# Two attention blocks: VectorE's weight subtractions moved up, fixed PSUM banks in the late rounds, GpSimd held at two points

## The reference

```python
h = rms_norm(x, attn_pre_norm[l])
proj = h @ w_in                      # 16 tiles of 128 columns, and tokens' values
o_fox = fox_attention(...)           # 4 heads, causal, with forget gates
o_dil = dilated_attention(...)       # 4 heads, three patterns
o_nsa = g0 * o_compressed + g1 * o_selected + g2 * o_window   # 8 heads, 2 kv groups
x = x + rms_norm(concat(o_fox, o_nsa, o_dil) @ w_out, attn_post_norm[l])
h = rms_norm(x, ffn_pre_norm[l])
x = x + rms_norm(conv_ffn(h), ffn_post_norm[l])
```

## Time and profile before

| | |
|---|---|
| median of 3 runs | 2835.21 us (2833.09 to 2837.86) |
| the profiled execution's own time | 2833.32 us |
| its span, first to last instruction | 2831.5 us |
| TensorE busy | 2719.4 us, 96% of the span |
| VectorE, ScalarE, GpSimd busy | 47%, 46%, 46% |
| mean granted TensorE clock | 0.993 of full |
| attention rounds and output product, layer 0 and 1 | about 2132 to 2264 us and 2496 to 2628 us |

### The profile page before, as it was taken

One profiled execution on the slowest core, in us unless ns is written; L12 is line 12 of the kernel. 1 busy time (PEld: TensorE's weight loads), 2 busy tenths in 40 slices (PEclk: granted clock), 3 DMA queues, 4 the chain that ended last, 5 costly groups with the idle time before them and its releaser, 6 DMA issues.

```text
span 2831.5 us, 42503 instructions
## 1 busy us (share of the span) xinstructions
PE 2719.4 (96%) x17634; PEld 2311.0 (82%) x17634; DVE 1329.0 (47%) x2629; ACT 1290.5 (46%) x2189; POOL 1294.6 (46%) x584
## 2 busy tenths in 40 slices
PE   7999999899999999999999999999999999999999
PEld 5777877688887687887878879989988699886997
DVE  2678867641333311103767664453126554156541
ACT  3254543423523522224464445654455566554664
POOL 3332021134442444442831428758860178720787
PEclk9999999999999999999999999999999999999999
DMA  6332012123233434334520215535553355543455
GB/s 244 103 130 101 31 67 82 53 99 117 90 127 122 164 134 149 118 99 148 180 82 16 83 61 179 171 108 185 178 194 118 114 160 182 166 145 112 151 184 156
DMA packets 104072, 361.40 MB, mean 128 GB/s; under 512 B 11142, under 2 KB 18566, under 8 KB 103368
## 3 DMA queue, kind: packets, MB, share of 16 engines
q1 hardware_dynamic: 103880, 358.68, 38.2%
HBM read 357.59 MB, written 1.05 MB: 127 GB/s over the span
## 4 chain that ended last, share of the span: by engine, by line
PE 83%; DVE 9%; ACT 4%; DMA 1%; POOL 1%; issue 1%; SPq 0%; DVEq 0%; ACTq 0%
PE PS L385 82%; DVE PS L2127 1%; DVE AR L2119 1%; ACT AR L1386 1%; DVE AR L2317 1%; POOL RINGL L2984 1%; DVE SM L2391 1%; ACT XT L1386 1%; DVE RINGL L2119 1%; PE PS L396 1%; DVE XT L2119 1%; DVE AR L2123 0%; POOL HTR L2989 0%; ACT L1386 0%; DVE AR L2410 0%
## 5 line engine op out<-in xcount | busy, mean ns | idle before, releaser
L2984 POOL TENSOR_TENSOR RINGL<-RING,WH 128x1024 fp32r<-128x1024 f32 x516 | 1229.3, 2395 | 1470.0 <-ACT WH L1366 1449.3
L1366 ACT ACTIVATE WH<-RING 128x1024 fp32r<-128x1024 f32 x548 | 569.5, 1045 | 689.9 <-PE PS L385 563.1
L385 PE MATMUL PS<-HTR,WH 128*128 128x256 f32 (+2 forms) x2736 | 805.9, 320 | 0.0
L385 PE MATMUL PS<-HTH,WH 128*128 128x256 f32 (+1 forms) x2336 | 681.3, 319 | 4.1 <-POOL HTR L2989 2.5
L385 PEld LDWEIGHTS PS<-HTR,WH 128*128 128x128 f32 (+1 forms) x2736 | 518.3, 190 | 39.6 <-issue 1.8
L385 PEld LDWEIGHTS PS<-HTH,WH 128*128 128x128 f32 x2336 | 443.7, 190 | 44.1 <-issue 14.4
L385 PE MATMUL PS<-ARR,WH 128*128 128x512 f32 (+1 forms) x1856 | 441.0, 340 | 3.5 <-ACT WH L1366 2.6
L385 PE MATMUL PS<-HTH,RINGL 128*128 128x256 f32 (+1 forms) x2336 | 403.6, 316 | 12.1 <-DVE RINGL L2119 9.8
L385 PEld LDWEIGHTS PS<-HTH,RINGL 128*128 128x128 f32 x2336 | 342.1, 191 | 43.0 <-DVE RINGL L2119 11.9
L385 PEld LDWEIGHTS PS<-ARR,WH 128*128 128x128 f32 x1856 | 311.0, 189 | 46.2 <-issue 5.6
L1386 ACT ACTIVATE AR<-PS 128x512 f32<-128x512 f32 (+6 forms) x344 | 163.4, 494 | 309.7 <-PE PS L385 298.2
(11 more groups left out here) (228 smaller groups left out, 3332.4 us busy)
## 6 DMA issues: line engine op xcount, KB each, us to landing
RING<-w_ada_in SPq DMA_DIRECT2D x96, 512.0 KB, 3.5
RING<-w_up_in SPq DMA_DIRECT2D x88, 512.0 KB, 3.6
RING<-w_gates_in SPq DMA_DIRECT2D x48, 512.0 KB, 3.4
RING<-w_ff_gate_in SPq DMA_DIRECT2D x44, 512.0 KB, 3.5
RING<-w_ff_up_in SPq DMA_DIRECT2D x44, 512.0 KB, 3.5
RING<-w_down_in SPq DMA_DIRECT2D x44, 512.0 KB, 3.6
RING<-w_glu_in SPq DMA_DIRECT2D x32, 512.0 KB, 5.4
RING<-w_ff_down_in SPq DMA_DIRECT2D x32, 512.0 KB, 3.5
```

The source lines that it names most:

```text
L385: return e.matmul(out_, lhsT, rhs, start=start, stop=stop)
L1366: e.activation(RINGS[name][:, j, 0:width], RING[:, b % NSLOT, 0:width], ACT.Copy).then_inc(*a_upper.up(b))
L2984: e.tensor_tensor(RINGL[:, i, 0:width], RING[:, i, 0:width], RINGS[name][:, j, 0:width], ALU.subtract).then_inc(*g_lower.up(b))
```

## The change

Three edits, all in the second block, once for each of its two layers. They add or remove no arithmetic.

1. VectorE's `lower_rows` for the block of round i+1 moves from the end of round i to just behind the maxima or the scaling.
2. From unit 14 on the scores of a pair always stand in banks 0 and 1; from unit 11 on all transposes stand in bank 2. Nothing of these takes from the turn any more, so the compressed branch's products take banks at other places of it.
3. GpSimd subtracts no block of `w_mix` before VectorE's last scaling (`weighed` of unit 23), and its second `w_up` block waits for the second diagonal instead of for the last residual.

```diff
@@ tensor: attention2
                 def weigh(u):
 
                     kind, _, q, k, v, o_, br, _ = UNITS[u]
+                    claim = (lambda par: take) if u < 14 else (lambda par: partial(bank, par))
                     both = [(u + par, slice(64 * par, 64 * par + 64),
-                             take("w2", l, u + par, until=(a_mix, "exp", l, u + par))) for par in range(2)]
+                             claim(par)("w2", l, u + par, until=(a_mix, "exp", l, u + par))) for par in range(2)]
...
                 def turn_over(u):
-                    o = take("t2", l, u, until=(d_mix if u % 2 else a_mix, "pb", l, u))
+                    claim = take if u < 11 else partial(bank, 2)
+                    o = claim("t2", l, u, until=(d_mix if u % 2 else a_mix, "pb", l, u))
@@ vector: attention2
                     if i < 24 and i % 2:
                         scale(i - 1)
+                    if i + 1 in TILE_AT:
+                        lower_rows("w_in2", TILE_AT[i + 1])
+                    if i + 1 in MIX_AT:
+                        lower_rows("w_mix", MIX_AT[i + 1])
                     if i - 1 in TILE_AT and TILE_AT[i - 1] in ROTATED:
                         rotate2(l, TILE_AT[i - 1])
...
-                    if i + 1 in TILE_AT:
-                        lower_rows("w_in2", TILE_AT[i + 1])
-                    if i + 1 in MIX_AT:
-                        lower_rows("w_mix", MIX_AT[i + 1])
@@ gpsimd
             for l in range(DEPTH):
                 for name in ("w_mix", "w_down")[0:2 - l]:
+                    if name == "w_mix":
+                        lowers(stage_block[name, l, 3] + 1)
+                        pool.wait_ge(*d_mix.to("weighed", l, 23))
                     lowers(stage_block[name, l] + 2)
-                    pool.wait_ge(*d_mix.to("xt", l, name, 1, 1))
+                    pool.wait_ge(*(d_norm.to("diag", l, 2, 1) if name == "w_mix" else d_mix.to("xt", l, name, 1, 1)))
```

More of the change, by code:

```diff
@@ L1 @@
 from contextlib import ExitStack
+from functools import partial
 import numpy as np
```

## The result

The changed kernel takes 2843.73 us (median of 8 runs, 2840.63 to 2850.11), the kernel before 2834.98 us in the same comparison. The ratio is 1.0035 with a 95% interval from 1.0025 to 1.0044: slower by a third of a per cent. The prediction was 2829 us, and its range ended at 2838. Its trace has a span of 2844.8 us (before 2831.5) and a mean granted clock of 0.984 (before 0.993).

What follows compares the result with a forecast made beforehand. TensorE, busy 96% of the span, was taken as the bound, so its waits count one for one. Per layer -5.3 + 4.2 - 1.8 + 0.6 = -2.3, twice -4.7, with the clock -6.3: 2835.2 to 2829 us, range 2818 to 2838.

Steps and rivals of the forecast that it cites:

- Edit 1, -5.3 a layer: Tile rounds: TensorE's five waits for VectorE's lower halves go, 4.9 us, plus some 0.1 us at each restart.
- Edit 2, +4.2 a layer: Late rounds: fixed banks make TensorE wait for exponentials and copies; together +4.2 us a layer, bounds +1 and +6.
- all six items: Late rounds' bank terms: `compress_fold` +1.8, round 15's copies +0.75, `compressed` +1.7, `compressed_over` -0.2, unit 18's transpose +0.7, unit 20's -0.6.
- Edit 3, the diagonal, -1.8 a layer and -1.6 once: Diagonals: GpSimd starting later shortens TensorE's wait, -1.8 us a layer; layer 0 keeps the clock there, -1.6 once.
- Edit 3, the hold, +0.6 a layer: Last scaling: GpSimd's released subtraction runs beside VectorE's last one; +0.6 us a layer, range 0 to 2.35.
- GpSimd's new start collides in full: VectorE's last subtraction waits a whole GpSimd instruction, 2.35 us a layer instead of 0.6; 2832.5 us, chance 0.10.
- The clock, 0: Late rounds: clock lost about as often as now; set at 0, with 3 us either way per layer.
- The clock pays: Late rounds: two new waits each pull the clock down, 1.6 us each, four times, +6.4; 2835 us, chance 0.15.
- One bank for all transposes: Units 11 to 23: 13 transposes a layer each wait behind a copy in bank 2; +16, 2845 us, chance 0.10.

Runs made afterwards that it cites:

- e1_move: The kernel before with only VectorE's `lower_rows` moved to just behind the maxima or scaling: 2817.61 us, ratio 0.9949.
- e6_last_banks: The kernel before with `lower_rows` moved, GpSimd's second-diagonal wait, and fixed banks only from unit 20 (scores) and 17 (transposes): 2810.77 us.
- e7_fill_waits: The changed kernel with 35 empty products a layer put into TensorE's five longest new waits: 2824.66 us, ratio 0.9973 to the kernel before.
- e10_turns_only: The changed kernel with only the transposes in a fixed bank, the scores' banks as before: 2820.73 us, ratio 0.9950 to the kernel before.
- e2_banks: The kernel before with only the fixed banks for scores and transposes: 2853.05 us, ratio 1.0072.
- e8_no_hold: The changed kernel without GpSimd's wait at VectorE's last scaling: 2830.48 us, ratio 0.9991 to the kernel before.
- e9_fold_free: The changed kernel with `compress_fold` in bank 2 instead of bank 0: 2833.13 us, ratio 0.9999 to the kernel before.

## Why the prediction was wrong

- **Edit 1, -5.3 a layer:** the mechanism held, and the size was a little low. No tile round waits for `RINGL`, and the stretch is 6.7 and 6.0 us shorter. In layer 0 the 0.46 us that TensorE waited for ScalarE ahead of unit 14's scores is gone as well, which I had not counted; in layer 1 it stays (0.41 before, 0.56 after). e1_move shows -14.5 us for the two layers, and a part of that is from its late rounds: `compressed_over` waits 1.18 us there instead of 1.9, and layer 1 has one loss of the clock less (64.2 to 60.1 us). I had put this at -0.2.
- **Edit 2, +4.2 a layer:** as waits, all six items are within 0.3 us of what I wrote. Fold 2.43 (2.5 forecast), the two behind it 0.36 and 0.28 together (0.75), `compressed` 1.66 (1.7), `compressed_over` 1.98 (1.7), the transpose of unit 18 0.65 (0.7), that of unit 20 1.22 (1.25).
- **Edit 3, the diagonal, -1.8 a layer and -1.6 once:** right, -3.3 and -1.7 us. Layer 0 kept the clock there.
- **Edit 3, the hold, +0.6 a layer:** mis-sized. The wait is 2.18 us, near the upper bound of 2.35 that I had written beside it. That is the fourth rival, "GpSimd's new start collides in full", which I gave 0.10. I had argued that TensorE has 2.4 us of products in between. It has them (2250.04 to 2252.44), but a microsecond of them runs before the last scaling ends at 2251.03, and the subtraction starts 0.18 us behind GpSimd's and takes 3.29 us. Besides, two blocks were waiting for GpSimd, and its two instructions took 5.69 us instead of 4.7.
- **The clock, 0:** this is the step that failed. I wrote "In the late rounds I expect the clock to be lost about as often as now" and kept 3 us either way. With the waits at 10.8 us in layer 0 instead of 4.7, TensorE is at the lower level for about 27 of the 75.7 us (1 less 0.82, twice, of 75.7). The work lost by that is at most 13.6 us, where it was 3.1 before (0.05 of 62.6). The other way round: at 1.00 the same work takes 52.5 us (e6_last_banks, layer 0). Of the changed kernel's 75.3 us, 10.8 are waits and so some 12.0 are the clock's; of the 60.1 before, 4.7 and 2.9. Where I had set 0, it is some 9 us more a layer. e7_fill_waits shows that the idle time of the waits is its cause: filled, they are as long, and the clock is at 1.00.
- **The rival "The clock pays"** had the mechanism, at 1.6 us a wait and two waits a layer. In the trace the waits add 6.1 us and the rest of layer 0's 15.2, some 9 us, is the clock, spread over four waits: about 2.3 each. The price of 1.6 came from one wait at the diagonals, 5.55 against 3.91 us for the same 32 products, and I took it for two waits and not for four.
- **"One bank for all transposes",** the only case that I put on the side of slower, is refuted by e10_turns_only. The result is slower by the sum of two other cases, each of which I priced alone and kept under the line: the collision 1.6 a layer above its term, the clock 9. I had no case for both together, though the collision is itself a wait that takes the clock.

What stays open: what makes a wait take the clock. Its length alone does not tell. In the kernel before, the wait ahead of `compressed_over` left the clock at 1.00 in layer 0 (1.93 us), and the same wait in layer 1 (1.92 us) was followed by 0.57. The 1.66 us ahead of `compressed` were followed by 0.56 in the changed kernel, and by 1.00 in layer 0 of e2_banks and of e8_no_hold. In e6_last_banks two waits of about 1.2 us left it at 1.00 in layer 0. No run varied what stands around a wait. So the 9 us are what these waits cost together in these traces, and not a fixed price of each.

## What to carry to other kernels

- When a change moves waits to other places in a stage of many short products like this one, price every wait of over a microsecond twice: its own length, and then the work at the lower clock behind it (here the added waits' 6.1 us came with some 9 us of it), unless the trace shows that the clock stays. The price of the clock belongs in the sum, not in the error bar; whether it is real is tested in one run, by filling the waits with empty products.
- Holding back an engine that shares SBUF moves its work, and so its collisions, to the moment of release, with a backlog. Ask what the other engine has in its queue at that moment; here it was the very subtraction that TensorE needed next.
- A bank taken in turn can be better than a fixed one: here the order of the turn had given `compress_fold` the one bank whose reader was long done.

## What was not expected of the hardware

- Adding 35 empty products to a stretch made it 12 us shorter (75.7 to 63.5 us), and doing so in both layers made the whole kernel 17.6 us shorter.
- The same wait in the same kernel can take the clock in one layer and leave it in the other (e9_fold_free: 2.20 us followed by 0.50 in layer 0, 2.18 us followed by 1.00 in layer 1).
- Twelve products of 15x256 take 1.45 us at the upper level of the clock and 2.60 us at the lower: 1.8 times as long.
- GpSimd's backlog of two subtractions blocked two VectorE instructions one after the other, 1.93 and 3.35 us for 0.41 and 1.22 us of work, and was itself hardly slowed by it (4.86 us for two, 2.35 for one alone). In the changed kernel it took 5.69 us for two, which fits VectorE's subtraction having run between them; that is read from the durations and not shown.
